# Norm rounds by token halves, and sixteen unread 512-column products after seven residuals

## The reference

```
def rms_norm(x, g):
    y = xf * lax.rsqrt(jnp.mean(xf * xf, axis=-1, keepdims=True) + EPS)
    return (y * g.astype(jnp.float32)).astype(x.dtype)

def modulate(x, g_pre, shift, scale):
    return rms_norm(x, g_pre) * (1 + scale) + shift

def residual_add(x, y, g_post, gate, res_w):
    return x + res_w * (1 + gate) * rms_norm(y, g_post)

h = modulate(x, norm_pre[l, 0], mod[:, 0, 0], mod[:, 0, 1])
x = residual_add(x, swiglu(h, ...), norm_post[l, 0], mod[:, 0, 2], 0.5)
```

## Time and profile before

| | us |
|---|---|
| three runs | 2413.7, 2414.21, 2417.6 |
| median | 2414.21 |
| the profiled execution | 2418.93 |
| its span, first to last instruction | 2416.9 |
| PE busy | 2180.3 |
| DVE busy | 1457.3 |
| ACT busy | 883.6 |
| POOL busy | 72.1 |
| mean granted TensorE clock | 0.955 of 2.4 GHz |

### The profile page before, as it was taken

The page is one execution under the profiler, slowest core; times in us unless marked ns, Lnnn a source line. Parts: engine busy times, 40 slices in busy tenths (PEclk is TensorE's granted clock), DMA queues, the critical chain, the costliest instruction groups (busy, mean ns, idle before and its releaser), DMA issues.

```text
span 2416.9 us, 28388 instructions
## 1 busy us (share of the span) xinstructions
PE 2180.3 (90%) x10492; PEld 1623.7 (67%) x10492; DVE 1457.3 (60%) x2214; ACT 883.6 (37%) x1093; POOL 72.1 (3%) x93
## 2 busy tenths in 40 slices
PE   2999899988998998999979998877999979889998
PEld 2788788866886886888857886655455467644553
DVE  6988677657886987766657986764122157532212
ACT  2343545534343343545534334421211244211111
POOL 0000000000000000000000001100000011000000
PEclk9999999999999999999989999877999989889999
DMA  8997443325995896444336983411999944139997
GB/s 347 379 375 303 148 164 145 137 111 224 361 372 197 323 380 254 149 156 148 131 127 246 363 360 129 143 51 53 354 394 396 407 180 171 48 134 382 385 388 295
DMA packets 86336, 592.64 MB, mean 245 GB/s; under 512 B 9680, under 2 KB 13136, under 8 KB 15568
## 3 DMA queue, kind: packets, MB, share of 16 engines
q1 hardware_dynamic: 79760, 579.90, 61.7%
q10 hardware_dynamic: 6464, 11.19, 1.4%
HBM read 590.00 MB, written 1.05 MB: 245 GB/s over the span
## 4 chain that ended last, share of the span: by engine, by line
PE 82%; DVE 9%; ACT 3%; DMA 2%; issue 2%; POOL 1%; DVEq 0%; SPq 0%; POOLq 0%; ACTq 0%
PE gu L2036 12%; PE tr L2036 11%; PE acc L1765 11%; PE acc L1769 10%; PE acc L1768 10%; PE gu L1765 6%; PE gu L1769 6%; PE gu L1768 6%; PE acc L2036 5%; PE tr L1809 3%; DVE w_lo L991 2%; DMA proj<-ada_stream 1%; DVE proj L1064 1%; DVE x_tok L1683 1%; PE tr L1817 1%
## 5 line engine op out<-in xcount | busy, mean ns | idle before, releaser
L991 DVE TENSOR_TENSOR w_lo<-stage,w_hi 128x2048 fp32r<-128x2048 f32 x240 | 548.0, 2287 | 77.5 <-ACT w_hi L526 77.4
L526 ACT ACTIVATE w_hi<-stage 128x2048 fp32r<-128x2048 f32 x240 | 457.3, 1911 | 296.2 <-PE acc L1769 272.8
L1064 DVE SCALAR_TENSOR_TENSOR proj<-proj,c_row 128x1024 f32<-128x1024 f32 x240 | 291.8, 1219 | 47.4 <-DMA proj<-ada_stream 37.2
L1765 PE MATMUL acc<-w_hi,hT_hi 128*128 128x512 f32 (+1 forms) x736 | 308.0, 418 | 9.1 <-DVE hT_lo L1353 5.1
L1768 PE MATMUL acc<-w_lo,hT_hi 128*128 128x512 f32 (+1 forms) x736 | 291.8, 397 | 0.0
L1769 PE MATMUL acc<-w_hi,hT_lo 128*128 128x512 f32 (+1 forms) x736 | 291.7, 396 | 0.0
L1765 PE MATMUL gu<-w_hi,hT_hi 128*128 128x512 f32 x704 | 279.5, 397 | 13.0 <-DVE pair L1132 8.8
L1769 PE MATMUL gu<-w_hi,hT_lo 128*128 128x512 f32 x704 | 274.8, 390 | 0.0
L1768 PE MATMUL gu<-w_lo,hT_hi 128*128 128x512 f32 x704 | 274.3, 390 | 0.0
L2036 PE MATMUL gu<-stage,got 128*64 128x512 f32 x1024 | 242.9, 607 | 1.6 <-DVE got L1205 1.6
L1765 PE MATMUL acc<-w_hi,yT_hi 128*128 128x512 f32 (+1 forms) x460 | 184.1, 400 | 14.0 <-DVE yT_lo L1565 5.7
(11 more groups left out here) (222 smaller groups left out, 2650.9 us busy)
## 6 DMA issues: line engine op xcount, KB each, us to landing
stage<-wstream SPq DMA_DIRECT2D x432, 1024.0 KB, 6.2
proj<-ada_stream SPq DMA_DIRECT2D x120, 1024.0 KB, 7.5
tf<-bgate_in ACTq DMA_DIRECT2D x12, 256.0 KB, 4.7
proj<-rel_in ACTq DMA_DIRECT2D x16, 192.0 KB, 2.3
proj<-t_in ACTq DMA_DIRECT2D x8, 192.0 KB, 2.4
z_mix<-c_in ACTq DMA_DIRECT2D x2, 512.0 KB, 5.3
x_tok<-x_in ACTq DMA_DIRECT2D x1, 1024.0 KB, 20.1
x_out<-x_tok SPq DMA_DIRECT2D x1, 1024.0 KB, 4.0
```

The costliest lines, as they stand in the source:

```text
L526: act.activation(w_hi[:, n % PARTS, :], stage[:, n % STAGES, :], ACT.Copy).then_inc(hi_ready, 1)
L991: dve.tensor_tensor(w_lo[:, n % PARTS, :], stage[:, n % STAGES, :], w_hi[:, n % PARTS, :].bitcast(F32), ALU.subtract).then_inc(chunk_ready, 1)
L1064: ins = dve.scalar_tensor_tensor(w, w, 1.0, c_row[:], ALU.mult, ALU.mult, accum_out=dst)
L1765: ins = pe.matmul(dst, l_hi, r_hi, start=start, stop=False, skip_group_check=True)
```

## The change

Rounds: round r now covers token half r // 2 and four of the eight column blocks (r % 2), with one diagonal only. DVE scales it in four operations of 128 columns instead of two of 256. The diagonal of half 0 is written inside the residual, after the multiply of half 1 and ahead of its add; that of half 1 at the head of the norm. `factors` moves to the start of the residual before. DVE's order in the norm is written out: scale 0, remainder 0, scale 1, scale 2, remainder 1, remainder 2, the split of the second chunk, scale 3, remainder 3. Except ahead of the router, PE runs round 3 after the first half of the first chunk, and each half of the first two chunks waits only for its own round.

Splits: `ahead` on DVE now splits one chunk, and the second goes into the norm; the rounded part of the third chunk is made by ACT inside the norm, too. At the start ACT sums the squares of `x_tok` before the first splits, DVE writes norm 0's diagonals ahead of modulation slice 6, and SP starts the weight chunks one slice later.

Products: after residuals 0 to 6 PE runs sixteen products of 512 columns into `gu`, which nobody reads.

```
@@ -460,7 +461,7 @@
-                if m >= NORM_SLICES - 3 and n < 8:
+                if m >= NORM_SLICES - 2 and n < 8:
                     chunk(n)
@@ act
-                    take_hi(b, 4, hT_hi, False)
+                    for r in range(4):
+                        t, half = r // 2, r % 2
+                        if r == 3 and (k < 3 * DEPTH or (k - 3 * DEPTH) % 2 == 0):
+                            hi(b["n"] + 2)
+                        act.wait_ge(tf_ready, b["tf"] + r + 1)
+                        act.activation(hT_hi[:, 4 * half:4 * half + 4, t * P:(t + 1) * P],
+                                       tf[:, (b["tf"] + r) % 2, :].rearrange("p (c s) -> p c s", c=4),
+                                       ACT.Copy).then_inc(th_ready, 1)
@@ dve, ahead
                 if n < n_chunks:
                     lo(n)
-                    lo(n + 1)
@@ dve
+            def root_diagonal(b, t):
+                dve.wait_ge(rs_done, b["req"] + t + 1)
+                dve.tensor_scalar(tok[:, t, 0:P], ident, rs[:, t:t + 1], None, ALU.mult).then_inc(src_ready, 1)
...
             for m in range(NORM_SLICES):
+                if m == NORM_SLICES - 2:
+                    dve.wait_ge(ld, 16 * N_LD)
+                    root_diagonal(plan[0][1], 0)
+                    root_diagonal(plan[0][1], 1)
@@ dve, norm
+                    if k:
+                        dve.wait_ge(x_ready, NT * k)
+                        root_diagonal(b, 1)
...
+                    scaled(0)
+                    rest(0)
+                    scaled(1)
+                    scaled(2)
+                    rest(1)
+                    rest(2)
+                    if k < 3 * DEPTH or (k - 3 * DEPTH) % 2 == 0:
+                        lo(b["n"] + 1)
+                    scaled(3)
+                    rest(3)
@@ dve, resid
                     dve.wait_ge(tr_free, b["u"] + 2)
+                    if k < NSUB - 1:
+                        factors(k + 1)
...
+                        if t and k < NSUB - 1:
+                            root_diagonal(plan[at + 1][1], 0)
                         dve.tensor_tensor(x[:, t, :], x[:, t, :], tok[:, 1, :], ALU.add).then_inc(x_ready, 1)
@@ pe
+            def norm_round(u, tf0, r):
+                t, half = r // 2, r % 2
+                pe.wait_ge(tf_ready, tf0 + r - 1) if r >= 2 else pe.wait_ge(tr_free, u + r + 1)
+                for j in range(4):
+                    c = 4 * half + j
+                    ins = small_mm(tr[:, (u + r) % 2, j * P:(j + 1) * P], x[:, t, c * P:(c + 1) * P], tok[:, t, 0:P])
+                ins.then_inc(tr_full, 1)
+
+            def normed(b, part):
+                def ready(t):
+                    if part == 0 and t == 1:
+                        norm_round(b["u"] - 4, b["tf"] - 4, 3)
+                    pe.wait_ge(tr_free, b["u"] - 1 + part + 2 * t)
+                return ready
...
+                elif kind == "resid" and step[1] <= 3 * DEPTH:
+                    for _ in range(WARM):
+                        pe.matmul(gu[:, 0, :], hT_hi[:, 0, 0:P], hT_hi[:, 0:2, :].rearrange("p a s -> p (a s)"), start=True, stop=True)
```

More of the change, by code:

```diff
@@ L927, in mixer @@
                 ahead(n0 + MIX_CHUNKS)
+            act.wait_ge(ld, 16 * N_LD)
+            for t in range(NT):
+                mean_square(plan[0][1], t, x[:, t, :], t)
             ahead(0)
@@ L1634, in mixer @@
                     lo(n0 + MIX_CHUNKS + s_ - SLOT_HEADS)
-            for step, b in plan:
+            factors(0)
+            for at, (step, b) in enumerate(plan):
                 kind = step[0]
@@ L1639, in _, with scaled, rest @@
                     k = step[1]
-                    dve.wait_ge(tr_free, b["u"] + 2)
-                    factors(k)
                     if k:
                         dve.wait_ge(x_ready, NT * k)
-                    for t in range(NT):
-                        dve.wait_ge(rs_done, b["req"] + t + 1)
-                        ins = dve.tensor_scalar(tok[:, t, 0:P], ident, rs[:, t:t + 1], None, ALU.mult)
-                    ins.then_inc(src_ready, 1)
-                    take_lo(b, 4, hT_hi, hT_lo,
-                            lambda c: (mod[:, 3 * k + 1, c:c + 1], mod[:, 3 * k, c:c + 1], ALU.add))
+                        root_diagonal(b, 1)
+                    def scaled(r):
+                        dve.wait_ge(tr_full, b["u"] + r + 1)
+                        if r >= 2:
+                            dve.wait_ge(tr_free, b["u"] + r + 1)
+                        for j in range(4):
+                            c = 4 * (r % 2) + j
+                            ins = dve.tensor_scalar(tf[:, (b["tf"] + r) % 2, j * P:(j + 1) * P],
+                                                    tr[:, (b["u"] + r) % 2, j * P:(j + 1) * P],
+                                                    mod[:, 3 * k + 1, c:c + 1], mod[:, 3 * k, c:c + 1], ALU.mult, ALU.add)
+                        ins.then_inc(tf_ready, 1)
+                    def rest(r):
+                        t, half = r // 2, r % 2
+                        at = (slice(None), slice(4 * half, 4 * half + 4), slice(t * P, (t + 1) * P))
+                        dve.wait_ge(th_ready, b["th"] + r + 1)
+                        dve.tensor_tensor(hT_lo[at], tf[:, (b["tf"] + r) % 2, :].rearrange("p (c s) -> p c s", c=4),
+                                          hT_hi[at].bitcast(F32), ALU.subtract).then_inc(tr_free, 1)
+                    scaled(0)
[8 more added lines that the diff above has]
+                    rest(3)
                 elif kind == "ffn" and not step[3]:
@@ L1772, in chunk_wait, with columns @@
                 pe.wait_ge(chunk_ready, n + 1 + STAGES * rounds * i)
-            def columns(n, dst, k0, kts, first, last, width=512, src=(hT_hi, hT_lo), i=0, pitch=512):
+            def norm_round(u, tf0, r):
+                t, half = r // 2, r % 2
+                pe.wait_ge(tf_ready, tf0 + r - 1) if r >= 2 else pe.wait_ge(tr_free, u + r + 1)
+                for j in range(4):
+                    c = 4 * half + j
[7 more added lines that the diff above has]
+                return ready
+            def columns(n, dst, k0, kts, first, last, width=512, src=(hT_hi, hT_lo), i=0, pitch=512, ready=None):
                 chunk_wait(n, i)
@@ L2121, in heads @@
                 for part in range(2):
-                    pe.wait_ge(tr_free, b["u"] + 2 * part)
-                    columns(n0 + part, lambda t: acc[:, t, :], 4 * part, 4, part == 0, part == 1)
+                    columns(n0 + part, lambda t: acc[:, t, :], 4 * part, 4, part == 0, part == 1, ready=normed(b, part))
                 for part in range(2):
@@ L2356, in _ @@
                 if kind == "norm":
-                    pe.wait_ge(src_ready, b["src"] + 1)
-                    for r in range(4):
-                        u = b["u"] + r
-                        pe.wait_ge(tf_ready, b["tf"] + r - 1) if r >= 2 else pe.wait_ge(tr_free, u + 1)
-                        for j in range(4):
-                            c, t = 2 * r + j // 2, j % 2
-                            ins = small_mm(tr[:, u % 2, j * P:(j + 1) * P], x[:, t, c * P:(c + 1) * P], tok[:, t, 0:P])
-                        ins.then_inc(tr_full, 1)
+                    for r in range(3 if step[1] < 3 * DEPTH or (step[1] - 3 * DEPTH) % 2 == 0 else 4):
+                        if r % 2 == 0:
+                            pe.wait_ge(src_ready, b["src"] + r // 2 + 1)
+                        norm_round(b["u"], b["tf"], r)
                 elif kind == "ffn" and not step[3]:
```

27 lines of the change are left out of this document (13 added, 14 removed).

## The result

The changed kernel took 2399.2 us (median of four runs, 2397.8 to 2403.7); the kernel before, on the same chip, 2414.75. The ratio is 0.9939, 95% interval 0.9926 to 0.9951: 0.6% faster, 15.6 us by the medians. The forecast was 2403.2, a gain of 10.95.

What follows compares the result with a forecast made beforehand. TensorE bounds the kernel, so only its idle time before the norms' products can be won. Gains of 15.6 and 2.25, less 2.0, 4.4 and 0.5, make 10.95 us off the 2414.2 median: 2403.2 us, range 2392 to 2413.

Steps and rivals of the forecast that it cites:

- Where the bound lies: TensorE is 82% of the chain; time can be won only where it idles, 112.3 us before the norms' products.
- (1): Ahead of the residual: one weight split fewer frees DVE 2.2 us earlier; after an FFN the first multiply starts about 1.1 earlier.
- (2): In the residual: first half's diagonal before the second add; second diagonal unchanged, 0.1 or 1.0 us later, after experts 0.7 earlier.
- (3): Norm rounds by halves: scaling pitch 0.33 us; gain 2.95 us where chunks are 512 wide, 2.0 for mixers, router norms lose 1.0.
- Rival E: DVE's queue between second diagonal and remainder 3: narrow scaling saves nothing, pitch 0.46 us; slower, 2419.5 us; chance 0.08.
- (4): Sixteen products after residuals 0 to 6: cost nothing, should give clock; clock drops in half of six norms, -4.4 us.
- Rival D: The products fail their purpose: rounds and the whole of half 0 run at 1.2 GHz; 2414 us, chance 0.07.
- Norm 8: Norm after the experts, no products there: 2.95 + 0.7, less 1.4 for a cold clock, gain 2.25 us.
- (5): Kernel start: first scaling at 39.5 to 41.8 instead of 42.13, later chunk queue paid in FFN 0; net -0.5 us.
- The sum: Norms 1 to 6 15.6, norm 8 2.25, norms 7 and 9 -2.0, clock -4.4, start -0.5: gain 10.95 us.
- the router's two norms: Norms 7 and 9: all four rounds needed, no overlap, diagonal 1.0 later; a loss of 1.0 us each.

Runs made afterwards that it cites:

- the gap filled: Changed kernel plus eight more unread 512-column products between rounds 1 and 2, for norms 0 to 6 and 8: 2392.2 us, ratio 0.9906.
- the experiment: Changed kernel with the old start (chunk loads behind slice 5, weight copies ahead of mean squares, norm 0's diagonals behind all eight slices): 2399.5 us, ratio 0.9938.

## Why the prediction was right, and where its terms were off

**Where the bound lies**: right. All the gain of norms 1 to 9 is idle time of PE ahead of the rounds and the first products. Two runs say what it hangs on: with the split ahead of the residual again 6.8 of the 14.4 us are gone, and without the overlap far more than all of them.

**(1) and (2), the residual.** The forecast had the second diagonal unchanged after an FFN, 0.1 later after the output projection, 1.0 later after the heads, 0.7 earlier after the experts. Measured behind the layer's end, before and after: 7.95 and 7.98, 7.85 and 7.97, 4.79 and 5.83, 11.47 and 10.69. Right four times. POOL's steps were 0.22 and 0.90 us (a fraction, and 1.13). The forecast told what the new wait costs, but did not ask what it would be without it; the diagonal behind the add was the larger gain.

POOL's first step takes 0.22 us, and 1.37, 1.13 or 0.90 where it comes up during a split or an add; it then ends 0.08 us behind the end of that DVE operation (240.88 + 1.37 against 237.67 + 4.50; 242.61 + 0.90 against 242.20 + 1.23 in the changed kernel). It waits until DVE's operation is over, rather than running slowly beside it. The Trainium skill, SBUF — State Buffer, section "SBUF: two separate sides", says that a GpSimd operation that reads SBUF and a VectorE operation with two SBUF inputs exclude each other for a whole instruction. The traces agree, also in that the multiply, which reads `acc` from PSUM, leaves the step at 0.22 (in the changed kernel at 244.70, beside the multiply of 244.27); that a port is the reason, no run here isolates.

**(3) Rounds by halves.** The pitch of a narrow scaling was taken at 0.33 us; four take 1.36 at a mean of 0.40 each, a pitch of 0.32. Remainder 3 was due at d+12.3 and ends at 11.8; the 48th product of a 512-wide norm at d+15.4, and where the clock holds it is 15.41 to 15.45. The mixers' gain was 2.0 and is 2.5 with the clock up. Rival E needed 0.42 and is out; doubling the scalings showed that a longer queue would have cost what it reckoned. Where no overlap was possible (norms 7 and 9) the loss was 0.65 instead of 1.0: the diagonal came 1.04 later, the chain behind it was 0.39 shorter. (The forecast wrote 9.8 us for that chain, where its own steps make 10.1; it measured 9.7.)

**(4) The clock.** The size was near, in part by luck: half of six norms at 1.4 us each (4.2; the forecast wrote 4.4), against 5.3 in five norms at 1.1 on average. More norms fell than forecast, each for less. The forecast named no row for its stretch of up to 3.4 us; the stretches over half 0 measured 3.4 us in four norms and 6.8 in norm 4. The mechanism was only half right. "They cost nothing" holds. "What they should give is clock" holds only for stretches that nobody waits for: the changed kernel without them is as fast. The step that failed reckons the loss by the part of the clock's fall that remains, and takes for granted that without the products more would be lost. Rival D had that the other way round and fell too: it priced every norm without a held clock at its whole gain, 15.6 us in all. What a fall over half 0 really costs is 0.5 to 1.4 us a norm. It is the gap ahead of round 2 that brings it, with or without products: 3.0 us idle there saw a fall over half 0 in five norms of six in both kernels, 1.7 us in three of six with products and in one without, and with the gap filled there was none. Which norms are spared changes from kernel to kernel.

**Norm 8**: 2.25 forecast, 3.78 measured. 0.78 is the diagonal and 3.0 the norm. The forecast took 1.4 off for a cold clock, but the norm was cold before too: its 48th product came at 19.05 then, 18.70 in norms 3 and 6. A cost that stands on both sides is no loss; what the cold clock takes there now is 0.6 (16.05, against 15.44 in the kernel with the gap filled, where the clock was back in time).

**(5) The start**: -0.5 forecast, +1.0 in the traces, nothing in the time of the experiment and 2.6 in its trace. The first scaling starts at 37.86, earlier than the 39.5 to 41.8 of the forecast. The forecast's sign was not confirmed; its bounds, -4 and +3, hold all of these.

**The sum**: terms that measured 11.9 (norms 1 to 6, clock in), 3.8, -1.3 and 1.0 make 15.4 where 10.95 was forecast. The 4.5 us between lie in norm 8 (1.5), the start (1.5), the router's two norms (0.7) and norms 1 to 6 (0.7), all on the same side. That the medians give 15.6 as well is chance: the spans, from which these terms are read, are 19.4 apart. The four microseconds beyond the terms are in layers where PE's instructions did not change. From a norm's 48th product to the layer's end, a later FFN took 179.1 us, but 179.9 to 181.4 once in each of five kernels, and a mixer 274.6 to 278.5. That they vary shows in the traces of kernels whose PE instructions differ only at the norms; why a given execution has the one or the other (the clock's falls in the sparse heads are the nearest candidate) was not isolated and stays open. It sets a floor of some 3 us under any verdict here.

## What to carry to other kernels

When two engines hand a result back and forth in rounds, cut it so that the consumer can start on the first part, and cut the work behind it to match. Here that needed narrower operations, 1.36 us a round instead of 1.00, and paid; the same cut with nothing run beside the rounds was 40 us slower than the kernel before. Ask of each long operation, too, whether it stands ahead of something waited for: one split moved out of the way is worth 6.8 of the 14.4 us at the norms. Dummy products hold a clock only if the gap that comes last before the real work is covered; look at the granted clock over the work that waits, not over the idle stretch, and try first to shorten that gap (here by moving one 0.3 us operation behind an add: 11 us by the medians, 7 of them seen at the norms). Before a cost is subtracted for a kernel after, check that the kernel before did not pay it as well.

## What was not expected of the hardware

A clock that falls early did less harm than one that was held up and fell later. With the first half's diagonal behind the add and no product at all, it fell in the idle stretch and was back at 2.4 GHz before the layer's first product in five of six norms. In the changed kernel the sixteen products kept it up through rounds 0 and 1, and it fell over half 0 in five of six. Part of that is the shorter gap; the like pair is the kernel with the diagonal moved and sixteen products, where the clock fell over half 0 in norms 1, 2 and 5 and norms 1 to 9 took 194.5 us, against 191.4 without products. By the medians these two are 1 us apart, which is not clear of noise. And the price of such a fall is smaller than the work that it slows: half 0 with its twelve products took 4.4 us in norm 3 of the changed kernel (first product to round 3) and 2.8 with the gap filled, and of these 1.6 us the 48th product came 1.3 later.
